# Long convolutions of one layer: another order of frequencies, transforms and token sums in four rounds

## The reference: what is computed

```python
def bidir_long_conv(u, h_fwd, h_bwd, bias):
    n = u.shape[1]
    lag0 = h_fwd[:1] + h_bwd[:1]
    k = jnp.concatenate([lag0, h_fwd[1:], jnp.zeros((1, C_WIDTH)), h_bwd[:0:-1]], axis=0)
    uf = jnp.fft.rfft(u, n=2 * n, axis=1)
    kf = jnp.fft.rfft(k, axis=0)
    y = jnp.fft.irfft(uf * kf[None], n=2 * n, axis=1)[:, :n]
    return y + u * bias
...
    for o in range(C_ORDER):                       # C_ORDER = 2, in hyena_mixer
        z = gx[o] * bidir_long_conv(z, filt[:, 0, o], filt[:, 1, o], filt_bias[o])
```

## Time and profile before

| what | us |
|---|---|
| median of 3 runs | 1894.63 (1893.53 to 1894.88) |
| the profiled execution's own time | 1894.86 |
| its span | 1893.0 |
| PE busy | 1832.6 (97%) |
| DVE busy | 824.6 (44%) |
| POOL busy | 66.1 (3%) |
| the four rounds and what joins them to the projection | 853 to 964 of the span |

### The profile page before, as it was taken

One profiled execution on the slowest core, in us unless ns is written; L12 is line 12 of the kernel. 1 busy time (PEld: TensorE's weight loads), 2 busy tenths in 40 slices (PEclk: granted clock), 3 DMA queues, 4 the chain that ended last, 5 costly groups with the idle time before them and its releaser, 6 DMA issues.

```text
span 1893.0 us, 18028 instructions
## 1 busy us (share of the span) xinstructions
PE 1832.6 (97%) x6829; PEld 962.7 (51%) x6829; DVE 824.6 (44%) x2070; ACT 411.4 (22%) x1011; POOL 66.1 (3%) x82
## 2 busy tenths in 40 slices
PE   6999999999999999998899999999999999999997
PEld 2545564444554744443345855588854443443432
DVE  4874545773865666536764234353432010010001
ACT  2121342101762221212212213212111111111111
POOL 0000000000000000004410000000010000000000
PEclk9999999999999999999999999999999999999999
DMA  9655100562100533411103330434396999999994
GB/s 401 253 210 184 45 1 33 201 217 94 68 1 30 191 118 149 148 75 44 73 1 144 123 130 4 173 121 165 143 377 264 428 428 427 427 428 428 428 428 167
DMA packets 31399, 367.57 MB, mean 194 GB/s; under 512 B 3676, under 2 KB 3789, under 8 KB 6349
## 3 DMA queue, kind: packets, MB, share of 16 engines
q1 hardware_dynamic: 31308, 366.36, 48.4%
HBM read 365.26 MB, written 1.09 MB: 194 GB/s over the span
## 4 chain that ended last, share of the span: by engine, by line
PE 92%; DVE 4%; issue 1%; ACT 1%; POOL 1%; DMA 1%; SPq 0%; DVEq 0%; POOLq 0%; ACTq 0%
PE bank L812 14%; PE bank L2951 12%; PE bank L714 9%; PE bank L1790 8%; PE bank L2988 6%; PE bank L1620 4%; PE bank L1337 3%; PE bank L2972 3%; PE bank L895 3%; PE bank L2926 3%; PE bank L2249 2%; PE bank L1465 2%; PE bank L917 2%; PE bank L1175 1%; PE bank L1503 1%; PE bank L2755 1%
## 5 line engine op out<-in xcount | busy, mean ns | idle before, releaser
L812 PE MATMUL bank<-hT,slot 128*128 128x256 f32 (+1 forms) x832 | 268.1, 478 | 0.4 <-DVE open_o L835 0.4
L812 PEld LDWEIGHTS bank<-hT,slot 128*128 128x128 f32 x832 | 156.0, 190 | 97.7 <-issue 85.0
L407 DVE SCALAR_TENSOR_TENSOR product<-slot,cond_rows 128x1024 f32<-128x1024 f32 x160 | 195.6, 1223 | 8.6 <-DVE product L407 2.8
L1790 PE MATMUL bank<-hT,slot 128*128 128x512 f32 (+1 forms) x448 | 168.9, 531 | 0.0
L714 PE MATMUL bank<-slot,gT 128*128 128x512 f32 x384 | 166.6, 592 | 0.0
L3028 DVE SCALAR_TENSOR_TENSOR hT<-hT,bank 128x512 f32<-128x512 f32 x16 | 11.0, 688 | 259.8 <-ACT hT L3063 259.8
L1790 PEld LDWEIGHTS bank<-hT,slot 128*128 128x128 f32 x448 | 83.2, 190 | 70.1 <-issue 67.0
L714 PEld LDWEIGHTS bank<-slot,gT 128*128 128x128 f32 x384 | 72.3, 190 | 88.0 <-issue 87.9
L2988 PE MATMUL bank<-slot,hT 128*64 128x512 f32 x256 | 92.1, 595 | 0.0
L2951 PE MATMUL bank<-slot,scratch 128*64 128x512 f32 x256 | 90.6, 592 | 0.0
L1620 PE MATMUL bank<-slot,hT 128*128 128x512 f32 x192 | 82.7, 592 | 0.0
(11 more groups left out here) (418 smaller groups left out, 2641.1 us busy)
## 6 DMA issues: line engine op xcount, KB each, us to landing
slot<-panels_dram SPq DMA_DIRECT2D x91, 2048.0 KB, 9.5
late_slots<-panels_dram SPq DMA_DIRECT2D x40, 2048.0 KB, 20.2
slot<-panels_dram SPq DMA_DIRECT2D x40, 1024.0 KB, 5.2
branch_slot<-panels_dram SPq DMA_DIRECT2D x9, 2048.0 KB, 23.3
mod_slot<-panels_dram SPq DMA_DIRECT2D x4, 2048.0 KB, 16.0
slot<-panels_dram SPq DMA_DIRECT2D x4, 1536.0 KB, 7.2
gate_rows_all<-gate_rows_dram SPq DMA_DIRECT2D x4, 1024.0 KB, 8.6
slot<-panels_dram SPq DMA_DIRECT2D x2, 1280.0 KB, 18.8
```

What stands on the lines that cost most here:

```text
L407: last = m.nc.vector.scalar_tensor_tensor(out=m.product[:], in0=m.slot(panel)[:, c * D:(c + 1) * D], scalar=1.0, in1=m.cond_rows[:, s, :], ...
L812: last = self.m.nc.tensor.matmul(self.bank(g), self.m.slot(panel)[:, k * width + j * P:k * width + (j + 1) * P], self.m.hT[:, k, 0:self.n] ...
L1790: last = nc.tensor.matmul(bank(g)[:, tokens], m.slot(i)[:, k * 512 + g % 4 * P:k * 512 + (g % 4 + 1) * P], m.hT[:, k, tokens], start=k == ...
```

## The change

Frequencies 1 and 3 go first everywhere: in the spectra, in the terms, in the transforms back and in DVE's `fold`, which now makes both differences first, then the odd sum, then the even one. The forward products of stream 0 for f = 1 and 3 move from after the spectra of round r+1 to the end of round r (in round 0 to before the spectra). The first two terms wait for three of the seven copies instead of all. There are three pairs of term buffers instead of two; the third uses the filter network's input tiles (now one tile, `ffn_in`) and a new tile `extra_term`. POOL's token sums of stream 1 move from the end of round r to the middle of round r+1.

```diff
@@ class Filters: fold
-        for n, (way, even_part) in enumerate(((even, True), (odd, False))):
...
+        for out, way in zip(self.differences, (even, odd)):
+            v.scalar_tensor_tensor(out=out, in0=way[:, 1, :], scalar=self.minus_but_first, in1=way[:, 0, :],
                                    op0=ALU.mult, op1=ALU.add).then_inc(self.folded.sem, self.folded.one())
+        for n, out, scaled, plain in ((2, self.sums[1], odd[:, 0, :], odd[:, 1, :]), (1, self.sums[0], even[:, 1, :], even[:, 0, :])):
+            dve.wait_ge(self.folded.sem, self.folded_at + 4 * r + n)
+            v.scalar_tensor_tensor(out=out, in0=scaled, scalar=self.but_first, in1=plain, op0=ALU.mult, op1=ALU.add) \
+                .then_inc(self.folded.sem, self.folded.one())
@@ conv_rounds
-    terms = m.scratch[:].rearrange("p b (h c) -> p b h c", h=2)
+    extra = m.sb("extra_term", [P, 512], own)
+    terms = [(m.scratch[:, b, 0:512], m.scratch[:, b, 512:]) for b in range(2)] + [(ffn_in[:], extra[:])]
+    DEEP = len(terms)
...
+    spectra = [(1, [(COSINE_ODD, filters.differences[0])]), (3, [(SINE_ODD, filters.sums[1])]),
+               (0, [(COSINE_EVEN, filters.sums[0]), (MIDDLE, filters.middle)]),
+               (2, [(LAST_COSINE, filters.sums[0]), (SINE_EVEN, filters.differences[1])])]
+    folds_before = {1: 1, 3: 3, 0: 4, 2: 4}
+    recipe = [(1, (1, 1), (3, 3), ALU.subtract), (3, (1, 3), (3, 1), ALU.add),
+              (2, (0, 2), (2, 4), ALU.add), (0, (0, 0), (2, 2), ALU.subtract)]
+    place = {1: 0, 3: 1, 0: 2, 2: 3}
+    forward_bank = lambda s, f: ps[4 * s + place[f]]
@@ tensor
+            def forward(r, s, some):
+                order, half = rounds[r]
+                if order == 1:
+                    pe.wait_ge(folded.sem, folded.at(2 * half + s + 1))
+                for f in some:
+                    nc.tensor.matmul(forward_bank(s, f)[:, :], dft[:, f, :], u[:, 2 * s + source[f], 0, cols(half)],
+                                     start=True, stop=True).then_inc(ready.sem, ready.one())
...
-                pe.wait_ge(filters.folded.sem, filters.folded_at + 4 * r + 2)
+                if r == 0:
+                    pe.wait_ge(filters.made.sem, filters.made_at + NX)
+                    forward(0, 0, (1, 3))
                 for g, parts in spectra:
-                    if g == 3:
-                        pe.wait_ge(filters.folded.sem, filters.folded_at + 4 * (r + 1))
+                    pe.wait_ge(filters.folded.sem, filters.folded_at + 4 * r + folds_before[g])
...
-                for s in range(2):
...
+                if r >= 1:
+                    pe.wait_ge(taken.sem, taken.at(2 * r))
+                forward(r, 0, (0, 2))
+                pe.wait_ge(copied.sem, copied.at(COPIES * (r + 1)))
+                forward(r, 1, (1, 3, 0, 2))
...
                     filters.products(pe, r + 1, 1, following)
                     inverse(r, 1, (2, 3))
+                    pe.wait_ge(taken.sem, taken.at(2 * r + 1))
+                    forward(r + 1, 0, (1, 3))
@@ vector
-                dve.wait_ge(copied.sem, copied.at(COPIES * (r + 1)))
+                dve.wait_ge(copied.sem, copied.at(COPIES * r + 3))
...
+                        if s == 0 and i == 2:
+                            dve.wait_ge(copied.sem, copied.at(COPIES * (r + 1)))
...
-                        if n >= 2:
-                            dve.wait_ge(combined.sem, combined.at(n - 1))
+                        if n >= DEEP:
+                            dve.wait_ge(combined.sem, combined.at(n - DEEP + 1))
@@ gpsimd
+                    if s == 0 and r >= 1 and rounds[r - 1][0] == 0:
+                        fold(r - 1, 1)
                 if order == 0:
-                    for s in range(2):
...
+                    fold(r, 0)
```

More of the change, by code:

```diff
@@ L1693, in conv_layer @@
             m.take(2, "c_decay", "c_w3")
[L1694 removed]
+            conv_rounds(m, mid, filters, dft, idft, kdft, u, ffn_in)
 ROUND = 1.5 * 2.0 ** 23
@@ L1950, in fold, with conv_rounds @@
         dve.wait_ge(self.made.sem, at)
-        for n, (way, even_part) in enumerate(((even, True), (odd, False))):
-            first, mirrored = way[:, 0, :], way[:, 1, :]
-            v.scalar_tensor_tensor(out=self.differences[n], in0=mirrored, scalar=self.minus_but_first, in1=first,
+        for out, way in zip(self.differences, (even, odd)):
+            v.scalar_tensor_tensor(out=out, in0=way[:, 1, :], scalar=self.minus_but_first, in1=way[:, 0, :],
                                    op0=ALU.mult, op1=ALU.add).then_inc(self.folded.sem, self.folded.one())
[L1955 to L1965, removed]
+        for n, out, scaled, plain in ((2, self.sums[1], odd[:, 0, :], odd[:, 1, :]), (1, self.sums[0], even[:, 1, :], even[:, 0, :])):
+            dve.wait_ge(self.folded.sem, self.folded_at + 4 * r + n)
+            v.scalar_tensor_tensor(out=out, in0=scaled, scalar=self.but_first, in1=plain, op0=ALU.mult, op1=ALU.add) \
+                .then_inc(self.folded.sem, self.folded.one())
+def conv_rounds(m, own, filters, dft, idft, kdft, u, ffn_in):
     nc, ps = m.nc, m.ps
@@ L2086, in _ @@
                         n = 2 * PER * r + PER * s + i
+                        if s == 0 and i == 2:
+                            dve.wait_ge(copied.sem, copied.at(COPIES * (r + 1)))
                         dve.wait_ge(ready.sem, ready.at(8 * r + 4 * s + 2 * (i // 2) + 2))
-                        if n >= 2:
-                            dve.wait_ge(combined.sem, combined.at(n - 1))
-                        nc.vector.tensor_tensor(terms[:, n % 2, 0, :], ps[4 * s + ua][:, :], spec[:, ka, :], ALU.mult)
-                        nc.vector.tensor_tensor(terms[:, n % 2, 1, :], ps[4 * s + ub][:, :], spec[:, kb, :], ALU.mult) \
+                        if n >= DEEP:
+                            dve.wait_ge(combined.sem, combined.at(n - DEEP + 1))
+                        first, second = terms[n % DEEP]
+                        nc.vector.tensor_tensor(first, forward_bank(s, ua)[:, :], spec[:, ka, :], ALU.mult)
+                        nc.vector.tensor_tensor(second, forward_bank(s, ub)[:, :], spec[:, kb, :], ALU.mult) \
                             .then_inc(scaled.sem, scaled.one())
@@ L2105, in _, with fold @@
         def _(pool):
+            def fold(r, s):
+                order, half = rounds[r]
+                first, second = (u[:, 2 * s + t, 1, cols(half)] for t in range(2))
+                pool.wait_ge(gated.sem, gated.at(2 * r + s + 1))
+                nc.gpsimd.tensor_tensor(u[:, 2 * s, 0, cols(half)], first, second, ALU.add)
+                nc.gpsimd.tensor_tensor(u[:, 2 * s + 1, 0, cols(half)], first, second, ALU.subtract) \
+                    .then_inc(folded.sem, folded.one())
             for r, (order, half) in enumerate(rounds):
@@ L2112, in _ @@
                         pool.wait_ge(scaled.sem, scaled.at(n + 1))
-                        nc.gpsimd.tensor_tensor(prod[:, s, f, :], terms[:, n % 2, 0, :], terms[:, n % 2, 1, :], op) \
-                            .then_inc(combined.sem, combined.one())
+                        first, second = terms[n % DEEP]
+                        nc.gpsimd.tensor_tensor(prod[:, s, f, :], first, second, op).then_inc(combined.sem, combined.one())
+                    if s == 0 and r >= 1 and rounds[r - 1][0] == 0:
+                        fold(r - 1, 1)
                 if order == 0:
-                    for s in range(2):
[L2117 to L2121, removed]
+                    fold(r, 0)
         @block.scalar
```

15 lines of the change are left out of this document (6 added, 9 removed).

## The result

| kernel | median us | runs | ratio to before, 95% interval |
|---|---|---|---|
| before | 1894.88 | 1893.53 to 1895.25 (5) | |
| changed | 1881.46 | 1880.42 to 1887.44 (5) | 0.9927 (0.9913 to 0.9940) |

The account below looks back on a forecast made before the run. No engine was full; a chain passing between engines bounded the rounds. Gains of 0.5, 3.9, 2.2 and 3.9 us in rounds 0 to 3, total 10.5, took 1894.86 to 1884.4; range 1880.5 to 1889.5.

Parts of the forecast that it names:

- fold, beside POOL: Start of DVE's fold until PE can use the odd sum, with POOL's token sum colliding: 3.26 us.
- fold, round 3: The same fold stretch in round 3, without the collision with POOL's token sum: 2.25 us.
- PE's 22 records: PE's unbroken row of spectra and forward products ahead of the next filter products: 9.72 us.
- pair and L1944: DVE's first filter pair and its extra row, 1.94 us, plus 0.25 for meeting POOL's later token sum.
- stream 1's terms: DVE's four terms of stream 1, no longer waiting for POOL with three buffers: 4.80 us, before 5.29 to 5.42.
- a middle round: Rounds 1 and 2, fold to fold: 24.59 us from the chain's links, 24.99 with the two new collisions.
- A new wait takes the place of the old one: Filter products wait for PE's own queue instead of DVE; about 1 us of what DVE wins is lost.
- Rival A: POOL and DVE miss each other at both middle folds, new collisions vanish: 2.8 us more gain, 1881.6; chance 0.15.
- Rival B: PE's lower clock returns during its waits, 1.7 us per fall: 1886.1 with one, 1889.5 with three; chance 0.17.
- Rival C: Expert-stage transfers starting at a fixed time swallow the whole gain: 1894.6 us; chance 0.05.
- Rival D: PE stays at its low clock level through the rounds, 86 chain records 0.43 us slower each: 1921; chance 0.05.
- 1.7 of the low clock not coming again: Part of round 1's 3.9 us gain: the slow first spectra seen once before would not recur, 1.7 us.

Follow-up runs that it names:

- before + third buffer: The kernel before with three pairs of term buffers and nothing else changed; stage 110.85 us, 105.77 without clock falls, 1899.58 us in one run.
- no forward ahead: The changed kernel with all four forward products of stream 0 behind their own round's spectra; stage 112.96 us, median 1897.97 us, ratio 0.9991 to before.

## Why the prediction was right

Its terms against the changed kernel's chain, for round 1 (875.07 to 900.17):

| term | predicted | measured |
|---|---|---|
| fold, beside POOL | 3.26 | 3.27 |
| fold, round 3 | 2.25 | 2.26 |
| PE's 22 records | 9.72 | 9.70 |
| filter products | 1.18 | 1.11 |
| pair and L1944 | 1.94 + 0.25 | 2.35 |
| stream 1's terms | 4.80 | 4.85 |
| `take` and pair | 3.69 + 0.15 | 3.82 |
| a middle round | 24.99 | 25.10 |

By round the gains were 0.65, 3.78, 2.08 and 3.80 against 0.5, 3.9, 2.2 and 3.9: 10.3 against 10.5. "A new wait takes the place of the old one" holds: DVE's 1.96 of idle time, and with the products moved ahead of it the wait shrinks to 1.23. By the Trainium skill's rule on the shared SBUF interface ("SBUF — State Buffer", "Who interferes with whom") I had put L1944's loss at 0.4, and 0.41 is what it lost; my 0.25 was too low. For the gate multiplication I had 0.2 by that rule, and 0.07 to 0.13 came.

What the stage doesn't give, 3.1 of the 13.4 us, lies in unchanged code and comes from where the clock fell; that is luck of this pair of executions. The forecast had no such term, and it is 2.9 over the measured median. On another chip, where each kernel ran several times, the medians lay 10.7 apart (1895.24 and 1884.54), close to the 10.5 of the forecast.

Rival A (no collisions) is out by the 2.44 of the differences, though its time, 1881.6, is the one nearest to the median: the number is right there by that luck, and not by the mechanism. Rival B (the lower clock again) did not come in the stage. Rival C (given back later) is out: the part after the stage is not longer, 927.80 against 928.45. Rival D (PE at the low level) did not come in any profile with the two products ahead: nine profiles, no fall in the stage. One reading made against it was wrong: I put PE at 21 of 25 us in a round and called it more than the 22.5 of 26.5 of before. These are the same share, 0.84 and 0.85; measured in the two windows it was 0.90 and 0.93.

One term was right for the profile that it was read from and too narrow for the kernel: the clock. I counted "1.7 of the low clock not coming again", one fall. In the four profiles without the move (two of before, before + third buffer, no forward ahead) there were nine falls in twelve places, 1.5 to 3.0 us each, and before itself had one and two. So the move saves 1.7 to 4.4 us by the clock, as the two profiles of before stand, beside its work on the chain; in the later measurements before ran from 1893.3 to 1901.2. How often each number of falls comes, these few profiles don't say.

## What to carry to other kernels

Where engines pass work round in a ring, sum one engine's queue between two waits, not only its busy share: PE was about 90% busy in the rounds and its order of 22 records still set the round. Here the work that was free to move paid twice where it broke TensorE's longest pause: 6.2 us on the chain, and the falls of the clock. And before moving a GpSimd job to a free place, look which VectorE instructions with two SBUF inputs stand there: against the sums at the round's end (99.60), one sum in the middle of the next round cost 0.8 us, and both sums behind the fold gained 2.0 (97.58).

## What the runs showed of the hardware

- A VectorE instruction on one partition (L1944, 1 x 512) is held up by GpSimd's 128-partition sum as a full one is: 0.68 alone, 1.09 and 1.82 beside it.
- Falls of the clock followed pauses of TensorE of 3.06 to 3.10 us in five of six places, and one of 2.2 us in one of three, in the three profiles with before's order. Without the two products ahead, pauses of 1.4 and 1.3 with 1.1 us of work between them did it in two of two places, and pauses of 1.4 and 0.3 in the one place that had them. In the nine profiles with the products ahead, no pause was over 1.6, and there was no fall in the stage.
- A fall costs 1.5 to 3.0 us here, as the spectra show: 5.42 became 6.92 to 8.28, and 4.56 became 6.26 and 7.51.
- Where VectorE and GpSimd met on SBUF inputs, the one that started second lost the time in these two cases: L1944, 0.7 behind the sum (890.47 against 889.75), took 1.09 for 0.68, and the sum kept its 1.28; the sum, 0.1 behind the gate multiplication (882.85 against 882.77), took 2.28 for 1.27, and the multiplication kept its 1.23.
